# Splits of the gate rows further ahead, alternating accumulators, and weight remainders on DVE in the plain part of a hybrid decoder layer

## Time and profile before

| | |
|---|---|
| median of 3 runs | 1576.38 us (1574.05 to 1578.75) |
| the profiled execution | 1574.16 us |
| its span, first to last instruction | 1572.4 us |
| granted TensorE clock, mean | 0.972 of full |
| busy share of the span | PE 94%, DVE 61%, ACT 44%, POOL 21% |

### The profile page before, as it was taken

One profiled execution on the slowest core, in us unless ns is written; L12 is line 12 of the kernel. 1 busy time (PEld: TensorE's weight loads), 2 busy tenths in 40 slices (PEclk: granted clock), 3 DMA queues, 4 the chain that ended last, 5 costly groups with the idle time before them and its releaser, 6 DMA issues.

```text
span 1572.4 us, 19428 instructions
## 1 busy us (share of the span) xinstructions
PE 1481.0 (94%) x7299; PEld 1240.3 (79%) x7299; DVE 954.4 (61%) x1305; ACT 685.4 (44%) x1231; POOL 333.4 (21%) x302
## 2 busy tenths in 40 slices
PE   5999999999989999998999999999899967699997
PEld 5777888788889998886778888888688855488885
DVE  5675445450178883668888888888833333223656
ACT  5433565222167873566644444444423331214334
POOL 3000000000077770143533333333000001000110
PEclk8999999999989999999999999999999987899998
DMA  7652425536133325454332222222454422223222
GB/s 217 84 91 33 48 86 161 143 94 122 59 102 104 106 87 182 153 159 126 100 98 80 81 80 81 81 80 81 173 208 147 141 99 88 90 84 108 94 90 99
DMA packets 147419, 170.76 MB, mean 109 GB/s; under 512 B 20408, under 2 KB 95358, under 8 KB 147326
## 3 DMA queue, kind: packets, MB, share of 16 engines
q1 hardware_dynamic: 147072, 169.41, 37.3%
q10 hardware_dynamic: 254, 0.10, 0.0%
HBM read 131.73 MB, written 37.75 MB: 108 GB/s over the span
## 4 chain that ended last, share of the span: by engine, by line
PE 87%; DVE 7%; ACT 3%; issue 1%; DMA 1%; POOL 0%; SPq 0%; ACTq 0%; DVEq 0%; POOLq 0%
PE psum L2081 10%; PE psum L2083 9%; PE psum L2082 9%; PE psum L2161 8%; PE psum L2163 8%; PE psum L2162 8%; PE psum L563 5%; PE psum L565 5%; PE psum L564 5%; PE psum L1202 4%; PE psum L1256 3%; PE psum L618 3%; PE psum L620 3%; PE psum L619 3%; ACT w_whi L142 1%
## 5 line engine op out<-in xcount | busy, mean ns | idle before, releaser
L148 DVE TENSOR_TENSOR w_wlo<-w_raw,w_whi 128x1024 fp32r<-128x1024 f32 x114 | 148.0, 1299 | 460.9 <-ACT w_whi L142 460.6
L142 ACT ACTIVATE w_whi<-w_raw 128x1024 fp32r<-128x1024 f32 x114 | 120.6, 1058 | 404.5 <-PE psum L2083 304.7
L2081 PE MATMUL psum<-w_whi,m_hi 128*128 128x512 f32 x544 | 220.1, 405 | 34.9 <-DVE m_lo L2880 34.9
L2083 PE MATMUL psum<-w_whi,m_lo 128*128 128x512 f32 x544 | 217.3, 399 | 0.0
L2082 PE MATMUL psum<-w_wlo,m_hi 128*128 128x512 f32 x544 | 217.2, 399 | 0.0
L2161 PE MATMUL psum<-m_hi,w_whi 128*128 128x512 f32 x416 | 163.2, 392 | 4.4 <-POOL w_wlo L1819 3.6
L2162 PE MATMUL psum<-m_lo,w_whi 128*128 128x512 f32 x416 | 162.4, 390 | 0.0
L2163 PE MATMUL psum<-m_hi,w_wlo 128*128 128x512 f32 x416 | 162.4, 390 | 0.0
L2081 PEld LDWEIGHTS psum<-w_whi,m_hi 128*128 128x128 f32 x544 | 105.9, 195 | 60.8 <-DVE m_lo L2880 38.7
L563 PE MATMUL psum<-h_hi,w_whi 128*128 128x512 f32 x320 | 126.9, 397 | 3.5 <-DVE h_lo L834 3.5
L565 PE MATMUL psum<-h_hi,w_wlo 128*128 128x512 f32 x320 | 125.4, 392 | 0.0
(11 more groups left out here) (353 smaller groups left out, 3106.1 us busy)
## 6 DMA issues: line engine op xcount, KB each, us to landing
w_raw<-in_w_down SPq DMA_DIRECT2D x44, 512.0 KB, 3.8
w_raw<-in_w_up SPq DMA_DIRECT2D x39, 512.0 KB, 3.9
w_raw<-in_w_in SPq DMA_DIRECT2D x36, 512.0 KB, 6.7
w_sums<-g_rows SPq DMA_DIRECT2D x44, 256.0 KB, 3.5
g_rows<-long_g SPq DMA_DIRECT2D x18, 512.0 KB, 2.6
w_raw<-in_w_out SPq DMA_DIRECT2D x16, 512.0 KB, 4.4
w_raw<-in_w_ple_gate SPq DMA_DIRECT2D x16, 512.0 KB, 3.8
w_more<-in_w_up SPq DMA_DIRECT2D x13, 512.0 KB, 3.8
```

Source lines behind the costliest of these rows:

```text
L142: act.activation(self.whi[self.ring(j)][:], self.raw[j % self.RAW][:], ACT.Copy).then_inc(self.rounded, 1)
L148: dve.tensor_tensor(self.wlo[self.ring(j)][:], self.raw[j % self.RAW][:], self.whi[self.ring(j)][:].bitcast(F32), ALU.subtract).then_inc(s ...
L2081: pe.matmul(out, ah, wh, start=(kt == first), stop=False)
L2083: ins = pe.matmul(out, al, wh, start=False, stop=(kt == last))
```

## The change

In neutral words, part by part:

- *Pieces 0 to 31 on DVE.* The remainders of the plain pieces move from POOL's queue to DVE's, where each has a written place (the new order of `dve_plain` is given in full below). POOL keeps the weight sums alone; its first one waits until six gate products are made, since its target is now also an accumulator.
- *Two sets of accumulators.* `short_acc` gives gate/up pairs n = 0, 2, 4, 6 the old buffers, n = 1, 3, 5 the buffer of the weight sums, and n = 7 a free raw buffer. The first tap of pair n waits for gate product n-2.
- *Norm of the second half.* Per row tile, `y*scale*row` then `x + y` become `y*row` (ahead of the reciprocal) then `y*scale + x`: four full-width instructions of each kind as before.
- *ACT's order in the plain part.* The repeated squares, the rounding of the sums and of the transposes are placed one or more tiles earlier; PE's transposes come after tiles 4 and 6.
- *Splits ahead.* `splits_at` gives the splits behind each slab: one up to down0's slab 18, then two each, so that behind slab i of down1 stand splits 26 + 2i and 27 + 2i. SP's loads of g rows are one further ahead. Splits 0 and 1 move into the last pair, ahead of DVE's last long_line addition; the remainder of down0's slab 1 moves ahead of the taps.

```diff
@@ Units.sum
+            if s == 0:
+                pool.wait_ge(gated, 2 * self.PLAIN - 2)
@@ Tail.__init__
+        odd, last = [sums[0][:, u, :] for u in range(2)], [self.hraw[:, 0, u, :] for u in range(2)]
+        self.short_acc = [([self.acc[0][:], self.acc[1][:]], odd)[n % 2] for n in range(2 * Units.PLAIN - 1)] + [last]
@@ Tail.sp
-            if kt + 1 < FT:
-                self.load_g(sp, kt + 1)
+            self.load_g(sp, kt + 1)
...
-            if i < FT // 2:
-                self.load_g(sp, FT + 2 * i)
-                self.load_g(sp, FT + 2 * i + 1)
+            for n in (FT + 2 * i + 1, FT + 2 * i + 2):
+                if n < 2 * FT:
+                    self.load_g(sp, n)
@@ Tail.pe_plain
-            if half == 0 and c in (5, 7):
+            if half == 0 and c in (4, 6):
@@ Tail.act, down0 and down1 (the same in Tail.dve)
-            self.act_split(act, kt + 2)
+            for n in self.splits_at(kt):
+                self.act_split(act, n)
...
-        self.act_split(act, FT + 1)
+        for n in self.splits_at(FT - 1):
+            self.act_split(act, n)
...
-            if i + 1 < FT // 2:
-                self.act_split(act, FT + 2 * i + 2)
-                self.act_split(act, FT + 2 * i + 3)
+            for n in self.splits_at(FT + i):
+                self.act_split(act, n)
@@ act_plain_line
-        act.wait_ge(self.s["gated"], n)
-        act.activation(self.acc[u][:], line[:, 0:HALF], ACT.Copy, scale=self.first_tap(n, u)).then_inc(self.s["tap0"], 1)
+        if n > 1:
+            act.wait_ge(self.s["gated"], n - 1)
+        act.activation(self.short_acc[n][u], line[:, 0:HALF], ACT.Copy, scale=self.first_tap(n, u)).then_inc(self.s["tap0"], 1)
@@ new
+    def splits_at(self, at):
+        if at < FT - 3:
+            return [at + 2]
+        if at < FT:
+            return [2 * at - FT + 5, 2 * at - FT + 6][:2 if at < FT - 1 else 1]
+        return [n for n in (2 * at - FT + 4, 2 * at - FT + 5) if n < 2 * FT]
@@ act_plain (c is the tile)
-            if c == last:
-                self.act_turn_first(act, 1, range(4, 8))
-            if c in (2, 3):
-                self.act_again(act, "outp1", 2 * (c - 2))
-                self.act_again(act, "outp1", 2 * (c - 2) + 1)
-            if c == 3:
+            if c == 2:
+                self.act_again(act, "outp1", 2)
+                self.act_again(act, "outp1", 3)
                 self.act_root(act, "outp1", 3, self.s["again_rooted"])
                 self.k.table(act, ACT.Silu)
...
             units.round(act, 2 * c + 4)
+            if c in (5, 7):
+                self.act_turn_first(act, 1, range(2 * (c - 5), 2 * (c - 5) + 4))
             if c:
                 self.act_plain_line(act, *divmod(c - 1, last))
-            if c == 4:
+            if c == 0:
                 self.act_sum1(act)
-            if c == 6:
-                self.act_turn_first(act, 1, range(4))
-            if c == 10:
-                self.act_sum23(act)
-            if c == 12:
+            if c == 1:
+                self.act_again(act, "outp1", 0)
+                self.act_again(act, "outp1", 1)
+            if c in (8, 9):
+                self.act_sum23(act, c - 8)
+            if c == 11:
                 self.act_sum4(act)
@@ act_pairs, last pair
                 self.slabs.round(act, self.first["down", 0], m)
+                self.act_split(act, 0)
+                self.act_split(act, 1)
...
         self.act_tap_gate(act, c)
-        self.act_split(act, 0)
-        self.act_split(act, 1)
@@ Tail.dve, after dve_turn_first(dve, 0, range(8))
+        self.units.remainder(dve, 0)
+        self.units.remainder(dve, 1)
         self.dve_out(dve, "outp1", 1, 1)
         self.dve_out(dve, "outp1", 3, 1)
+        self.units.remainder(dve, 2)
@@ dve_pairs, last pair
                 self.slabs.remainder(dve, self.first["down", 0])
+                self.dve_split(dve, 0)
+                self.dve_split(dve, 1)
             m.wait(dve, p3)
...
         self.dve_join(dve, Units.PAIRS - 1, Units.T4)
-        self.dve_taps(dve, last, 0, self.long_acc[1], self.long_line[1], 1)
         self.slabs.remainder(dve, self.first["down", 0] + 1)
-        self.dve_taps(dve, last, 1, self.long_acc[0], self.long_line[0], 0)
-        self.dve_split(dve, 0)
-        self.dve_split(dve, 1)
+        self.dve_taps(dve, last, 0, self.long_acc[1][:], self.long_line[1], 1)
+        self.dve_taps(dve, last, 1, self.long_acc[0][:], self.long_line[0], 0)
         self.dve_gate(dve, last)
@@ Tail.pool
-        for n in range(3):
-            units.remainder(pool, n)
-        for n in range(3, Units.N_PLAIN):
-            if n == Units.N_PLAIN - 2:
-                units.sum(pool, 0, Units.T1)
-                units.sum(pool, 0, Units.T2)
-            units.remainder(pool, n)
+        units.sum(pool, 0, Units.T1, self.s["gated"])
+        units.sum(pool, 0, Units.T2)
```

More of the change, by code:

```diff
@@ L1770, in used, with sum @@
             eng.wait_ge(self.made, 4 * s + 4)
-    def sum(self, pool, s, which):
+    def sum(self, pool, s, which, gated=None):
         if s >= self.PAIRS:
@@ L2423, in act_sum1, with act_sum23 @@
             act.activation(self.s1[:, 0, kt, :], self.hraw[:, 1, kt, :], ACT.Copy).then_inc(self.s["sum_hi"], 1)
-    def act_sum23(self, act):
+    def act_sum23(self, act, which):
         act.wait_ge(self.s["x_out"], 16 * NT)
[L2427 to L2431, removed]
+        for kt in range(KT // 2):
+            self.banks.released(act, ("f1", kt))
+            act.activation(self.s23[:, 2 * which, kt, :], self.hraw[:, 1 - which, kt, :],
+                           ACT.Copy).then_inc(self.s["sum_hi"], 1)
     def act_sum4(self, act):
@@ L2622, in dve_scale, with dve_row_first, dve_scale_add @@
                                  op1=ALU.mult).then_inc(self.s["scaled"], 1)
+    def dve_row_first(self, dve, i):
+        y = self.y["outp1"][:, i, :]
+        dve.wait_ge(self.s["squared"], self.square_of["outp1", i])
+        dve.wait_ge(self.s["norm_rows"], 32)
+        dve.tensor_tensor(y, y, self.wrow[0][:], ALU.mult).then_inc(self.s["scaled"], 1)
+    def dve_scale_add(self, dve, i):
+        t = self.HT + i
+        dve.wait_ge(self.x_arrived[t], 16)
+        dve.wait_ge(self.s["scaled"], self.HT + i + 1)
+        dve.scalar_tensor_tensor(out=self.x[:, t, :], in0=self.y["outp1"][:, i, :], scalar=self.column(2, "outp1", i),
+                                 in1=self.x[:, t, :], op0=ALU.mult, op1=ALU.add).then_inc(self.added[i % 2], 1)
     def add(self, eng, post, i):
@@ L2696, in dve @@
             slabs.remainder(dve, j + i + 2)
-            if i + 1 < FT // 2:
-                self.dve_split(dve, FT + 2 * i + 2)
-                self.dve_split(dve, FT + 2 * i + 3)
+            for n in self.splits_at(FT + i):
+                self.dve_split(dve, n)
             if i == 2:
@@ L2883, in dve_plain @@
         before, units = "outp1", self.units
-        taps = lambda n, u: self.dve_taps(dve, n, u, self.acc[u], self.line[u], u)
+        taps = lambda n, u: self.dve_taps(dve, n, u, self.short_acc[n][u], self.line[u], u)
         gate = lambda n: self.dve_gate(dve, n)
-        self.dve_invert(dve, before)
-        for i in range(self.HT):
-            self.dve_scale(dve, before, i)
-            self.add(dve, before, i)
+        rest = lambda first, source, hi, lo: self.dve_sum_rest(dve, first, source, hi, lo)
@@ L2890, in dve_plain @@
+        piece = lambda n: units.remainder(dve, n)
+        self.dve_row_first(dve, 0)
+        self.dve_row_first(dve, 1)
+        piece(3)
+        self.dve_row_first(dve, 2)
+        self.dve_row_first(dve, 3)
+        self.dve_invert(dve, before)
+        self.dve_scale_add(dve, 0)
+        piece(4)
+        self.dve_scale_add(dve, 1)
+        piece(5)
+        self.dve_scale_add(dve, 2)
+        piece(6)
+        self.dve_scale_add(dve, 3)
+        piece(7)
         taps(0, 0)
+        piece(8)
@@ L2891, in dve_plain @@
         taps(0, 1)
+        piece(9)
         self.dve_divide(dve, before)
+        piece(10)
+        rest(0, 1, lambda kt: self.s1[:, 0, kt, :], lambda kt: self.s1[:, 1, kt, :])
         gate(0)
         taps(1, 0)
+        piece(11)
         taps(1, 1)
-        self.dve_sum_rest(dve, 0, 1, lambda kt: self.s1[:, 0, kt, :], lambda kt: self.s1[:, 1, kt, :])
+        piece(12)
         gate(1)
+        self.dve_turn_first(dve, 1, range(2))
+        piece(13)
+        piece(14)
+        self.dve_turn_first(dve, 1, range(2, 4))
@@ L2898, in dve_plain @@
         taps(2, 0)
-        self.dve_turn_first(dve, 1, range(4))
+        piece(15)
+        piece(16)
         taps(2, 1)
+        self.dve_turn_first(dve, 1, range(4, 8))
+        piece(17)
+        piece(18)
         gate(2)
-        self.dve_turn_first(dve, 1, range(4, 8))
         taps(3, 0)
+        piece(19)
+        rest(4, 1, lambda kt: self.s23[:, 0, kt, :], lambda kt: self.s23[:, 1, kt, :])
+        piece(20)
         taps(3, 1)
+        self.dve_sum4(dve)
+        piece(21)
         gate(3)
```

(37 more changed lines are left out.)

35 lines of the change are left out of this document (19 added, 16 removed).

## The result

The changed kernel takes 1502.53 us (median of 4 runs, 1501.58 to 1504.49) against 1575.37 us for the kernel before (4 runs). The ratio is 0.9536, 95% interval 0.9517 to 0.9555. The profiled execution took 1504.49 us with a span of 1502.8 us.

What follows compares the result with a forecast made beforehand. PE, busy 94% of the span, was taken as the bound, with only its waits and lower clock to win. Gains of 59.0 + 7.3 + 7.5 + 0.6 = 74.4 us from 1574.16, plus 2.2, gave 1502.0 us; range 1493 to 1511.

Steps and rivals of the forecast that it cites:

- Down1: First 11 slabs of down1: splits made two slabs ahead cut 120.8 us to 61.8, a gain of 59.0 us.
- The chain of 3.6 us: Down1: ACT's and DVE's work after each slab takes 3.6 us and now has 5.44, a margin of 1.8 us.
- The 2 us for POOL's additions: Down1: POOL's two additions for down0 lengthen DVE remainders beside them, costing between 0 and 3 us; 2 taken.
- The seam: Between pairs and down0: splits 0 and 1 made earlier cut 15.0 us to 7.7, a gain of 7.3 us.
- the two g rows are there: Between pairs and down0: slab 0 can start as the pairs end, its weights and two g rows being there.
- The recorded sum for slab 2: Start of down0: gate product ends near 1143.0, then 1.2 for slab 2's remainder and 0.7 for split 2: 1144.9.
- The 1.9 us: Down0: PE is ready for slab 2 at 1143.06 and stalls 1.9 us until its inputs are made.
- The plain part: Plain pieces: remainders on DVE and a second accumulator set cut 101.1 us to 93.6, a gain of 7.5 us.
- DVE as the bound: Rival, plain part: DVE's added remainders make the stage 111 us instead of 93.6, total 1519 to 1520; chance 0.08.
- nets nothing: Rival, plain part: DVE's relief from POOL equals its added work, PE waits as before, total 1509.5; chance 0.06.
- The kept stalls of down1: Rival, down1: ACT, DVE and POOL meet in 5.44 us steps, 15 us come back, total 1517; chance 0.10.
- the slower side: Rival, down1: SP's single queue brings loads just in time and all gains are lost, 1581; chance 0.02.

Runs made afterwards that it cites:

- e1: The kernel before with only the splits and SP's g loads of down0 and down1 further ahead: 1517.35 us.
- e2: The changed kernel with the splits of down1 one row less far ahead, one of two still made after the slab before: 1549.13 us.
- e3: The changed kernel with all four residual additions of down0 on DVE, none on POOL: 1500.26 us.
- e8: The changed kernel with down0's additions on DVE, g rows 0 and 1 loaded early, and slab 2's and piece 0's work placed sooner: 1494.55 us.
- e7: The changed kernel with SP's loads of g rows 0 and 1 issued before the store of the last but one g row: 1498.95 us.
- e4: The changed kernel with the remainders of pieces 0 to 31 back in POOL's queue: 1506.74 us.
- e9: The changed kernel with the remainders of pieces 0 to 31 back on POOL and one set of accumulators: 1512.07 us.
- e5: The changed kernel with one set of accumulators again, so pair n's first tap waits for gate product n-1: 1504.77 us.

## Why the prediction was right

It gave 1502.0 and 1502.53 was measured. What it says of the causes is borne out by the runs; that the total agrees to 0.5 us is in part luck, as the end of this section shows. By steps:

- **Down1**, 59.0 forecast, 57.9 measured; e1 shows it by itself. The chain of 3.6 us fits under 5.44, as e2 shows from the other side: with one of two splits back in the chain the stall and the fall of the clock are back. The 2 us for POOL's additions measured 2.2, and e3 shows that they were the cause. The floor was 60.3 us and not 59.8, since three slabs run slower at the full clock (last section). The loads cost nothing at 167 GB/s. ACT's and DVE's other work (squares, table, scalings) never made PE wait in e3.
- **The seam** is the term that was mis-sized: 7.3 forecast, 4.0 measured, at the lower of the bounds of 4 and 9.6. The step that failed is "the two g rows are there". I took them as landed when ACT came to them; they landed some 5 us after their issue, which SP makes behind a store and a slab. So the wait before slab 2 was 3.09 us, not 1.9, and slab 0 waited 0.17. The clock's part was off as well: 0.4 was taken, and 125.2 - 119.7 - 3.3 = 2.2 measured, against e8 with no wait. e7 shows the first as the cause. The recorded sum for slab 2 doesn't close either: 1141.6 - 1.3 + 1.5 is 1141.8, and it says 1143.0. On the time scale of the kernel before, the gate product ended at 1145.0 in the changed kernel and at 1142.1 in e7, where the g rows were there. The 1.9 us thus held about 1 us too much for the queues and nothing for the g rows, and the two errors partly cancel.
- **The plain part**, 7.5 forecast, 8.1 measured. The two waits that I named by walking the order are in the trace where I put them: 0.72 us before piece 0 (0.8 forecast), 0.60 before piece 13 (0.5). The profile names no releaser for the first; it is absent in e8, which makes that remainder sooner. DVE is busy for 84.3 of 93.0 us; the bound was 88. That its older work would shrink by about what the pieces add was the assumption on which this rested, and e4 shows it from the other side, with 87.3 us busy for 32 instructions fewer. What I had not seen is how far the two halves of this part cover for each other: of the 10.2 us between e9 and the changed kernel, the remainders on DVE bring 7.1 by themselves (e5) and the second accumulator set 6.3 (e4).
- **The rivals.** DVE as the bound and "nets nothing" both fall with e4: PE waits less with the remainders on DVE. The Trainium skill's rule (Perfetto Trace Analysis, Optimizing Scalar/DVE Operations), that moving work between GpSimd and DVE "might not help" since they share a port, did not decide this case: the move helped by 3.9 to 7.1 us, as the remainder is twice as long on POOL (1.3 to 0.68 us) and DVE's own instructions take longer beside it. The kept stalls of down1 were 1.6 us, not 15. Nothing came near the slower side.

Of the signs that the prediction named, those for down1 held (62.6 us, waits of 1.6 us, a clock of 1.00, none ended by a DMA or SP). Others held only nearly: the wait before slab 2 was 3.09 us (1 to 3), there was one of 0.17 before slab 0 (none), DVE was busy for 84.3 us (85 to 90), and two of its additions of a tap took 0.84 and 1.67 us (never above 0.8).

The total agrees better than its terms do. From profile to profile the forecast was 74.4 us and 69.7 were gained: the seam gave 3.3 us less, down1 1.1 less, the plain part 0.6 more, and 1.2 us were lost ahead of the change. Against this, the profiled execution after was 2 us above its own median, where the profiled one of before was 2 below the median that the forecast was scaled by. This scatter between executions hid the difference.

## What to carry to other kernels

Where a ring is two deep and the conversions for the next step are issued behind the end of this one, count in steps, not in us: what matters is whether anything that step i + 1 needs stands behind the end of step i. The last split of 0.6 us there was worth 47 of 57 us (e2 beside the changed kernel), since it stood behind a rounding and a remainder, and since here the clock fell with each of the ten pauses. When an operation is moved from GpSimd to VectorE, price VectorE's present work without its neighbour before adding the moved one. After such a change look at once for what now meets in shorter steps: here two residual additions, two late loads and the places of slab 2's and piece 0's work were together worth another 8 us.

## What the runs showed of the hardware

- Beside a POOL instruction with SBUF inputs, DVE instructions of several forms took longer by about what was left of it, and not by a share: the 1.23 us slab remainder took 3.40 and 3.41 us, 2.2 more, beside additions of 3.31 and 3.30 that had 2.3 us left. The scaling with a single SBUF tensor input took longer too (6.62 us for four, 2.74 without). The Trainium skill (SBUF — State Buffer, Who interferes with whom) describes both forms; the trace agrees.
- Pauses of nearly the same length cost the clock differently. Pauses of 3.07 us before each of ten slabs left it at 0.84 (e2). After the single one of 3.09 us at the seam PE was back at the full clock for six matmuls and only then fell to 0.43 us a matmul for seven. In e3 a shorter one, 2.61 us at the same place, was followed by seven at 0.43 us too, but after 2.94 us in e4 and 2.77 us in e9 none was slow. So the length of the pause alone doesn't tell what it costs. Pauses of 0.41 and 1.20 us left 1.00.
- Matmuls whose stationary operand is in `g_last` start 0.233 us apart and not 0.227, at a clock of 1.00; the timeline of PE in the changed kernel, three matmuls apart:

```profile
1299.62 0.39 PE L2084 MATMUL psum<-w_whi,g_last 128*128 128x512 f32 x1
...
1300.32 0.39 PE L2084 MATMUL psum<-w_whi,g_last 128*128 128x512 f32 x1
```

It makes the three slabs 0.16 us longer each. The first nine matmuls of the next slab, which don't read `g_last`, are 0.23 us apart too (1312.22 to 1314.30 in the same timeline), so that the buffer is not the whole of it. No run here tells the cause.
